# Raw halves in front of the root: leading units of three normed products in a two-block transformer kernel

## What is computed

```python
def rms_norm_2(x, g):
    xf = x.astype(jnp.float32)
    y = xf * lax.rsqrt(jnp.mean(xf * xf, axis=-1, keepdims=True) + EPS)
    return (y * g.astype(jnp.float32)).astype(x.dtype)

def modulate(h, shift, scale):
    return h * (1.0 + scale[:, None, :]) + shift[:, None, :]

def swiglu(h, w_gate, w_up, w_down):
    return (jax.nn.silu(h @ w_gate) * (h @ w_up)) @ w_down

# per layer i:
    h = modulate(rms_norm_2(x, ffn_norm[i, 0]), mod[:, 0, 0], mod[:, 0, 1])
    x = x + 0.5 * mod[:, 0, 2][:, None, :] * swiglu(h, ...)
    h = modulate(rms_norm_2(x, mix_norm[i]), mod[:, 1, 0], mod[:, 1, 1])
    y = conv_mixers(h, ...)       # layer 0; pool_moba_mixers(h, ...) in layer 1: z = h @ w_in, then u, q, k, v
    x = x + mod[:, 1, 2][:, None, :] * y
```

## Time and profile before

| | us |
|---|---|
| median of 3 runs | 1812.28 |
| lowest and highest | 1807.25, 1812.35 |
| the profiled execution | 1812.7 |
| its span | 1810.9 |

### The profile page before, as it was taken

The page is one execution under the profiler, slowest core; times in us unless marked ns, Lnnn a source line. Parts: engine busy times, 40 slices in busy tenths (PEclk is TensorE's granted clock), DMA queues, the critical chain, the costliest instruction groups (busy, mean ns, idle before and its releaser), DMA issues.

```text
span 1810.9 us, 34579 instructions
## 1 busy us (share of the span) xinstructions
PE 1766.4 (98%) x14098; PEld 1570.8 (87%) x14098; DVE 1380.5 (76%) x2297; ACT 1032.2 (57%) x1747; POOL 85.3 (5%) x163
## 2 busy tenths in 40 slices
PE   7999999989999999999999999999999999999998
PEld 6888889888888888888888888888888888988887
DVE  4758888767766478888888967688979887767664
ACT  3557764667766577654655412655555555466553
POOL 0000001100000000001001100010100010000000
PEclk9999999999999999999999999999999999999999
DMA  5356558443332356568788933788968887536552
GB/s 193 94 186 205 190 200 325 128 141 118 119 96 95 116 183 204 187 221 316 266 282 286 348 117 116 257 295 285 332 239 309 277 318 243 171 118 210 190 192 94
DMA packets 102827, 374.04 MB, mean 207 GB/s; under 512 B 11440, under 2 KB 11600, under 8 KB 102544
## 3 DMA queue, kind: packets, MB, share of 16 engines
q1 hardware_dynamic: 80352, 289.77, 46.8%
q0 software_dynamic: 22320, 82.09, 13.5%
HBM read 370.74 MB, written 1.08 MB: 205 GB/s over the span
## 4 chain that ended last, share of the span: by engine, by line
PE 92%; ACT 3%; DVE 3%; issue 1%; DMA 0%; SPq 0%; DVEq 0%; ACTq 0%
PE ps L520 40%; PE ps L523 22%; PE ps L2169 4%; PE ps L527 3%; PE ps L528 3%; PE ps L529 3%; PE ps L611 2%; PE ps L898 2%; PE ps L1083 1%; PE ps L2195 1%; PE ps L1264 1%; PE ps L1265 1%; PE ps L1266 1%; PE ps L317 1%; PE ps L1384 1%
## 5 line engine op out<-in xcount | busy, mean ns | idle before, releaser
L491 DVE TENSOR_TENSOR weights_lo<-weight_ring,weights_hi 128x1024 fp32r<-128x1024 f32 x493 | 602.3, 1223 | 158.3 <-ACT weights_hi L484 157.3
L484 ACT ACTIVATE weights_hi<-weight_ring 128x1024 fp32r<-128x1024 f32 x493 | 517.4, 1054 | 196.8 <-PE ps L520 120.2
L520 PE MATMUL ps<-u_halves,weights_hi 128*128 128x512 f32 x2176 | 536.7, 391 | 2.3 <-DVE u_halves L379 1.8
L520 PEld LDWEIGHTS ps<-u_halves,weights_hi 128*128 128x128 f32 x2176 | 400.3, 188 | 83.5 <-DVE u_halves L379 3.4
L523 PE MATMUL ps<-u_halves,weights_lo 128*128 128x256 f32 x2176 | 304.5, 283 | 0.0
L523 PEld LDWEIGHTS ps<-u_halves,weights_lo 128*128 128x128 f32 x2176 | 288.1, 191 | 10.1
L520 PE MATMUL ps<-act_halves,weights_hi 128*128 128x512 f32 x952 | 231.3, 391 | 0.0
L520 PEld LDWEIGHTS ps<-act_halves,weights_hi 128*128 128x128 f32 x952 | 173.5, 188 | 32.4
L721 DVE SCALAR_TENSOR_TENSOR ffn_tiles<-ffn_tiles,cond 128x1024 f32<-128x1024 f32 x144 | 175.4, 1220 | 3.0 <-DMA ffn_tiles<-in_ada 2.8
L633 ACT ACTIVATE ffn_tiles<-ps 128x512 f32<-128x512 f32 x136 | 80.8, 594 | 157.6 <-PE ps L523 157.4
L527 PE MATMUL ps<-u_halves,weights_hi 128*128 128x256 f32 x488 | 147.3, 302 | 4.9 <-DVE u L1887 2.9
(11 more groups left out here) (312 smaller groups left out, 2148.2 us busy)
## 6 DMA issues: line engine op xcount, KB each, us to landing
weight_ring<-in_w SPq DMA_DIRECT2D x545, 512.0 KB, 4.1
ffn_tiles<-in_ada POOLq DMA_DIRECT2D x144, 512.0 KB, 5.4
scaled<-gates_scratch POOLq DMA_DIRECT2D x8, 512.0 KB, 5.5
arena<-in_alibi POOLq DMA_DIRECT2D x1, 1536.0 KB, 6.9
h<-in_x SPq DMA_DIRECT2D x4, 256.0 KB, 3.9
out<-u SPq DMA_DIRECT2D x4, 256.0 KB, 2.4
consts<-in_consts SPq DMA_DIRECT2D x1, 592.0 KB, 10.2
cond<-in_cond SPq DMA_DIRECT2D x1, 512.0 KB, 11.2
```

Of the source, the lines that this page charges most:

```text
L484: nc.scalar.activation(w_slot(s)[0], ring[:, n % RING], ACT.Copy).then_inc(hi_ready, 1)
L491: nc.vector.tensor_tensor(lo, ring[:, n % RING], hi.bitcast(F32), ALU.subtract).then_inc(lo_ready, 1)
L520: return nc.tensor.matmul(ps[:, bank], hi, halves, start=start, stop=stop, skip_group_check=True)
```

## The change

At norms 4, 7 and 8 (`RAW`) the first four units (SPLIT) are multiplied with halves of h times norm weight, without the root. `lead_hi_act` makes the high half in the place of `scaled`, `lead_lo_dve` the low half right behind the sum of squares of the same chunk. The halves of the shift stand as columns 256 and 257 of the same tiles (`PITCH` = 258), so the products (`lead_pe`) have 258 columns, three for each chunk of a unit, and one unit follows another. Behind the fifth chunk of the first unit stands `norm_pe`, now with all eight squares summed on DVE and one ones-matmul, without warming matmuls. The results are multiplied by `rstd` on DVE (`lead_scale_dve`; in `moba_dve` in place in PSUM) and the shift's product is added as a bias (in the Silu, in `mul_dve`, in the pool copy). `norm_dve` and `norm_halves_act` still make the normed halves, which units 4 and on use. The fourth unit's weights are split before the root; the fifth's high half stands between chunks 3 and 4 of `norm_halves_act`. `ADA_DOWN` moves modulation sums away from the last chunk.

The diff, cut to its core:

```diff
+        RAW = (4, 7, 8)
+        GAIN_WITH_ROOT = (0, 1, 9) + RAW
+        AFTER = {3: 1, 4: 2, 6: 3, 7: 4, 8: "pm_in"}
...
+        def lead_hi_act(act, k, c):
+            if c == 0 and k in MODS:
...
+                nc.scalar.activation(lead_halves(k)[:, :, 0, T:PITCH], shift, ACT.Copy).then_inc(shift_hi_ready, 1)
+            nc.scalar.activation(lead_halves(k)[:, c, 0, 0:T], h[:, c], ACT.Copy, scale=norm_gain(k, c)).then_inc(lead_hi_ready, 1)
...
+            dve.wait_ge(lead_hi_ready, leads_until(k, c))
+            nc.vector.scalar_tensor_tensor(lead[:, c, 1, 0:T], h[:, c], norm_gain(k, c), lead[:, c, 0, 0:T].bitcast(F32),
+                                           ALU.mult, ALU.subtract).then_inc(lead_lo_ready, 1)
...
+        def lead_pe(pe, k):
...
+            for j in range(SPLIT):
+                s = split_wait(pe, AFTER[k], j)
+                pe.wait_ge(h_ready, C * (k - 1) + lead_bank_read(k, j))
+                for c in range(C):
+                    if j == 0:
+                        pe.wait_ge(lead_lo_ready, leads_until(k, c))
+                    nc.tensor.matmul(ps[:, j, 0:n], w_hi[:, s, c], lead[:, c, 0, 0:n], start=c == 0, stop=False, skip_group_check=True)
+                    nc.tensor.matmul(ps[:, j, 0:n], w_hi[:, s, c], lead[:, c, 1, 0:n], start=False, stop=False, skip_group_check=True)
+                    last = nc.tensor.matmul(ps[:, j, 0:n], w_lo[:, s, c], lead[:, c, 0, 0:n], start=False, stop=c == C - 1, skip_group_check=True)
+                    if j == 0 and c == SUM_BEHIND:
+                        norm_pe(pe, k)
+                last.then_inc(unit_done, 1)
+
+        SUM_BEHIND = 4
...
         def norm_halves_act(act, k):
             for c in range(C):
+                if k in RAW and c == C // 2:
+                    split_hi(act, AFTER[k], SPLIT)
...
+        ADDED.update((k, C) for k in RAW)
...
-            if k in WARM:
+            if k in WARM and k not in RAW:
                 warm_pe(6, WARM[k])
...
-        ADA_DOWN = [[3] + [2] * 6 + [1]] * 2 + [[3] * 3 + [2] * 4 + [1], [3] + [2] * 6 + [1], [2] * 4 + [1] * 4, [0] * C]
+        ADA_DOWN = [[3] + [2] * 6 + [1], [3] * 2 + [2] * 5 + [0], [3] * 3 + [2] * 4 + [1], [3] + [2] * 6 + [0], [2] * 6 + [1] + [0], [0] * C]
...
         def corr_act(act, q, f):
+            if f < 2 and k_raw(q):
+                return
...
+            if k + 1 in RAW:
+                split_hi(act, AFTER[k + 1], SPLIT - 1)
             norm_root_act(act, k + 1)
...
+        def lead_scale_dve(dve, q, f):
+
+            unit_products(dve, FIRST_UNIT[f"ffn{q}"], 2 * f + 1)
+            if FFN[q][0] in MODS:
+                nc.vector.tensor_copy(lead_bias[:, 2 * f:2 * f + 2], ps[:, 2 * f:2 * f + 2, T])
+            root2 = rstd[:].unsqueeze(1).to_broadcast([P, 2, T])
+            nc.vector.tensor_tensor(gu[:, f % 3], ps[:, 2 * f:2 * f + 2, 0:T], root2, ALU.mult).then_inc(gu_ready, 1)
...
                 add_squares_dve(dve, k + 1, c - 1)
+                if c and k + 1 in RAW:
+                    lead_lo_dve(dve, k + 1, c - 1)
                 ffn_residual_dve(dve, steps, q, c)
...
+            if k + 1 in RAW:
+                add_squares_dve(dve, k + 1, C - 1)
+                lead_lo_dve(dve, k + 1, C - 1)
             if piece > bias_from:
                 mods_bias_dve(dve, bias_from, piece)
+            if k + 1 in RAW:
+                split_lo(dve, AFTER[k + 1], SPLIT - 1)
...
         def moba_pe(pe):
...
+            lead_pe(pe, 8)
+            for n in range(SPLIT, 12):
...
                 if n == 8:
+                    pe.wait_ge(p_copied, 4)
                     scores_pe(pe, 1, 0)
...
                 if n < 4:
+                    if n:
+                        split_hi(act, "pm_in", n + 4)
+                    act.wait_ge(p_scaled, n + 1)
+                    nc.scalar.activation(px[:, n, PADP:PADP + T], ps[:, n, 0:T], ACT.Identity, bias=lead_bias[:, n:n + 1]).then_inc(p_copied, 1)
+                    continue
...
+            split_lo(dve, "pm_in", 4)
+            for n in range(SPLIT):
+                unit_products(dve, FIRST_UNIT["pm_in"], n)
+                nc.vector.tensor_copy(lead_bias[:, n:n + 1], ps[:, n, T:T + 1])
+                nc.vector.tensor_tensor(ps[:, n, 0:T], ps[:, n, 0:T], rstd[:], ALU.mult).then_inc(p_scaled, 1)
+                if n == 1:
+                    split_lo(dve, "pm_in", 5)
+            split_lo(dve, "pm_in", 6)
+            split_lo(dve, "pm_in", 7)
```

More of the change, by code:

```diff
@@ L130, in build @@
         u = sb("u", [P, C, T])
+        PITCH = T + 2
+        with nc.sbuf_tensor("lead_in_mix", [P, C, 2, PITCH], FR) as lead_in_mix:
+            pass
         with nc.sbuf_tensor("mix_halves", [P, 2 * C, T], FR) as mix_halves:
@@ new lines, in lead_bank_read @@
+        def lead_bank_read(k, j):
+            if k == 3:
+                return 2 * j + 2
+            if k == 6:
+                return (7, 8, 2, 4)[j]
+            return 5 + j
+        def lead_pe(pe, k):
+            lead, n = lead_halves(k), PITCH if k in MODS else T
+            if k in MODS:
+                pe.wait_ge(shift_lo_ready, shifts_until(k))
+            for j in range(SPLIT):
[10 more added lines that the diff above has]
+                last.then_inc(unit_done, 1)
@@ L394, in residual_dve @@
                 split_lo(dve, next_ffn, 0)
+            raw = k + 1 in RAW
             for c in range(C):
-                if banks != "lin":
+                if banks != "lin" and not raw:
                     add_squares_dve(dve, k + 1, c - 1)
@@ L559, in ffn_up_pe @@
                         begin, end = first and c == 0, not first and c == C - 1
+                        if j == SPLIT and first and k in RAW:
+                            pe.wait_ge(u_hi_ready if part == "low" else u_lo_ready, 8 * HALVES_OF[k] + c + 1)
+                        elif j == SPLIT and k in RAW:
+                            pe.wait_ge(u_lo_ready, 8 * HALVES_OF[k] + c + 1)
                         if part == "high":
@@ L621, in ffn_pe, with k_raw, corrs_until @@
             ffn_down_pe(pe, q)
-            norm_pe(pe, FFN[q][0] + 1)
+            if FFN[q][0] + 1 not in RAW:
+                norm_pe(pe, FFN[q][0] + 1)
         def has_split(q, j):
             return j < 3 * FFN[q][1] + {0: GDN_SPLIT, 1: SPLIT - 1, 3: SPLIT - 1, 4: SPLIT - 1}.get(q, 0)
+        def k_raw(q):
+            return FFN[q][0] in RAW
+        def corrs_until(q, f):
+            return F_BASE[q] + f + 1 - 2 * sum(k_raw(i) for i in range(q + 1))
         def corr_act(act, q, f):
+            if f < 2 and k_raw(q):
+                return
             unit_products(act, FIRST_UNIT[f"ffn{q}"], 2 * f + 1)
@@ L644, in silu_act @@
                 act.wait_ge(act_ready, n - 2)
-            nc.scalar.activation(sgb[:, f % 2], src, ACT.Silu).then_inc(sg_ready, 1)
+            bias = lead_bias[:, 2 * f:2 * f + 1] if f < 2 and k_raw(q) and FFN[q][0] in MODS else 0.0
+            nc.scalar.activation(sgb[:, f % 2], src, ACT.Silu, bias=bias).then_inc(sg_ready, 1)
         def act_hi_act(act, q, f):
@@ L2490, in moba_dve @@
                 m(nc.vector.memset(b[:, :, 0:PADP], 0.0))
-            for n in range(4, 8):
-                split_lo(dve, "pm_in", n)
+            split_lo(dve, "pm_in", 4)
[7 more added lines that the diff above has]
+            split_lo(dve, "pm_in", 7)
             w()
```

105 lines of the change are left out of this document (71 added, 34 removed).

## The result

| | before | changed |
|---|---|---|
| median, us | 1812.28 | 1802.15 |
| lowest and highest of 7 runs, us | 1807.25, 1813.72 | 1798.79, 1803.63 |
| ratio, with its 95% interval | | 0.9945 [0.9935, 0.9956] |
| span of the profiled execution, us | 1810.9 | 1800.4 |
| mean granted clock | 0.995 | 0.996 |

What follows compares the result with a forecast made beforehand. PE's stream of products and its stops were taken as the bound. Savings of 3.35, 3.4 and 3.1 us at norms 4, 7 and 8, taken as 9.8, gave 1802.9 from 1812.7, then 1802.5 us for the runs; range 1797.5 to 1809.5.

Steps and rivals of the forecast that it cites:

- What bounds the kernel: PE's stream of products plus its stops; at norms 4, 7 and 8 together 12.83 us pass without a product.
- The products: Four lead units at each norm: 96 products of 258 columns at 0.121 us, 11.6 us against 11.14 at norms 4 and 7.
- Rival B: The 288 lead products of 258 columns are slower than rows of 256, up to +29 us, 1831 us; chance 0.07.
- Unit 0: First lead unit: PE does not stop, with 0.2 us to spare at the sum and 1 us at step 7.
- PE is free at 1337.84: At norm 7, after the last down product: the time from which the lead was taken to start.
- Rival C: The sum of squares inside unit 0 stops PE; 1 us per norm returns, 1805.5 us; chance 0.08.
- Unit 4: First unit on normed halves, the tightest place: PE waits about 0.15 us; 3.35, 3.4 and 3.1 us saved at norms 4, 7, 8.
- The root: On ACT, unit 3's split put before the root costs nothing, since the ones-matmul releases the root at the same time, 1340.4.
- Unit 5 at norm 8: ACT waits for the scaled pool input before it splits unit 5: another 0.1 us.
- Moved load: Extra DVE work in the down stages, 3.2 us each, and moved modulation sums: costed at nothing; without cover up to 3.2 us per norm.
- rival A: DVE takes the chain's place, in down stages or at unit 4's weights: 1.5 to 3.2 us per norm; chance 0.13.
- The total: Whole kernel: 9.8 us off the profiled 1812.7 gives 1802.9, with the runs' median 0.4 lower, 1802.5 us.

Runs made afterwards that it cites:

- experiments 1 to 3: Kernel before with only the change's SBUF addresses, 1811.82 us, ratio 1.0004; then the changed kernel with the lead at fewer norms, raw78 and raw8.
- Experiment 7: Changed kernel with tiles of pitch 256 and the lead as products of 512 and 256 columns, without the shift: 1803.75 us, ratio 0.996 to the kernel before.
- experiment 8: Changed kernel with each low half of the lead made twice on DVE, once into an unread tile: 1803.96 us, ratio 0.9954 to the kernel before.
- experiment 4: Changed kernel with the ones-matmul behind the eighth chunk of unit 0 in place of the fifth: 1804.53 us, ratio 0.9962 to the kernel before.
- Experiment 6: Changed kernel with unit 4's low half made before DVE's eighth norm chunk and, at norm 8, unit 5 split before the first pool copy: 1801.47 us.
- after_again: The changed kernel measured once more, nothing altered: 1803.63 us against 1810.88 for the kernel before, ratio 0.9956.
- raw78: Changed kernel with the lead at norms 7 and 8 only, norm 4 put back: 1804.6 us against 1811.3 for the kernel before, ratio 0.9971.
- raw8: Changed kernel with the lead at norm 8 only, norms 4 and 7 put back: 1808.04 us against 1811.3 for the kernel before, ratio 0.9978.

## Why the prediction was right, and where it was not

**What bounds the kernel**: right. PE's stream was stopped in the three stretches, and the gain is found at the norms that have the lead and nowhere else (experiments 1 to 3). One loss elsewhere, between norms 5 and 6, comes below.

**The products**: 288 products of 258 columns at 0.121 us were predicted; the lead takes 12.09 us with its ones-matmul (1333.48 to 1345.45 and one product more), against 12.1. Rival B, slower products, is excluded. Experiment 7 adds what the prediction didn't see: their price was not on the path at all, for unit 4 starts at the same time with the cheaper form. The price was also too high. In experiment 7 it is 0.17 us a lead in place of 0.46, since products of 512 and 256 columns that alternate take 0.354 us a step (21 steps from 1342.46 to 1349.89, before) and 0.357 in experiment 7, and not the 0.348 of the groups in rows 8. The sum didn't suffer, for it compares with the measured 11.37 us.

**Unit 0**: predicted 0.2 us of margin for the sum of squares and no stop. The profile names no stop, but the margin is gone: the ones-matmul is released by the sum, 0.08 us late at norm 7 (experiment 8). The step at fault is "PE is free at 1337.84". PE was free 0.18 us earlier, and the lead reaches the sum that much sooner. Rival C did not happen, but its place is real and close.

**Unit 4** was named the tightest place, and it is. The prediction has unit 4 start at 1350.1, 13.40 us behind the start of the last down products; measured are 13.43, 13.48 and 13.65. That fits at norms 4 and 7, where 3.35 and 3.4 us were predicted and 3.32 came, but with luck, for terms are off and nearly cancel. The lead starts 0.18 us earlier than was taken. PE stops for 0.43 us and not 0.15. And DVE's norm is longer: 6.6 us from the trace of before plus 0.6 for the inserted split, 7.2, and measured are 7.38 (1337.28 to `half_gate`'s start at 1344.66). The 6.6 were of `norm_dve` on `scaled`, a TENSOR_TENSOR of 0.42 us. With the lead there is no `scaled` made on ACT, and the diff shows it: `GAIN_WITH_ROOT` takes in `RAW`, so the operation becomes a SCALAR_TENSOR_TENSOR with the gain, 0.48 us (L435), 0.40 from start to start (1338.80 to 1339.20) in place of 0.34 (0.42 less the overlap of 0.08). Eight times 0.06 is 0.5 us, and it was in the diff to be read. The inserted split, on the other hand, delayed DVE by 0.34 us (before 1342.00) and not by 0.6. The two misses, +0.5 and -0.26, are about the 0.2 us by which the norm is longer; it starts 4.76 us behind the last down products where 4.85 was predicted.

At norm 8, where 13.78 was predicted (1539.2 - 1525.42), unit 4 starts after 13.65, and the start before was taken 0.16 us too early (1542.38 for 1542.54): 3.47 us in place of the 3.2 that the prediction has before it takes off 0.1 for unit 5.

**The root**: "that insertion costs nothing: the two end together" was right. In experiment 4, where nothing else holds it, the root starts 0.63 us after the ones-matmul (1333.26 to 1333.89), here 0.71, so the split holds it by at most 0.1; and rstd is ready 0.25 us before DVE can use it.

**Unit 5 at norm 8**: predicted 0.1 us late. The stretch from norm 8 to the end gained 3.10 us where unit 4's start has 3.47, so 0.4 was given back behind it. The profile names no wait there, but the starts show it: unit 5's first product is 0.15 us late, where 0.1 was predicted, and the second product behind each stop costs 0.10 more. Experiment 6 gets all of it back, 0.9 us with the 0.60 before unit 4.

**Moved load**, costed at nothing in the down stages: right, with a cover that is used up at twice the load (rival A's price shows at norm 7 only, in experiment 8). Not right on one point that the sum didn't have: in the stage between norms 5 and 6 the changed kernel loses 0.4 to 0.5 us. It is 105.4 and 105.3 us (after_again) against 104.9, and 104.6 in raw78 and raw8, whose sums for the modulation are placed as in the changed kernel. There PE has one new wait, in the mixer between these norms:

```profile
1089.25 1.12 PE L2318 MATMUL ps<-arena,consts 128*128 128x512 f32 x2 [0.41 <-DVE arena L2409]
```

It appears with 0.3 to 0.4 us in all six profiles of kernels with a lead at norm 4, and neither before nor in raw78 or raw8. In five of the six the wait before the mixer's first product (for ACT) is also 0.7 us in place of 0.4; in the sixth, two_products, it isn't, and there the stage takes 105.0. What makes DVE and ACT late there was not tried, and stays open.

**The total**: 1802.5 predicted, 1802.15 measured, and this agreement is better than the working behind it. By the stages the norms gave 9.6 us in place of 9.85, the mixer took 0.4 to 0.5 back, and the stretch before norm 4 gave 1.45 us that the change has no part in. Without that the gain is 9.05 us, and the profiled execution would have taken 1803.65 us, against 1802.9 that the sum gave: an error of some 0.75 us. The second measurement of the same kernel, 1803.63 us, lies there, 7.25 us below its own runs of before (1810.88), where the first lies 10.13 below.

## What to carry to other kernels

Where an engine shows 98% busy, look at what the busy time is made of: three stretches of 4.3 us were filled with matmuls that nobody read, and products that don't need the result being waited for took their place. Once such a gap is closed, the end is set by what was hidden behind it, here DVE's norm and one weight half: count it with the operations of the changed code, not with those of the trace before, and look there first for the next gain (some 0.5 us at norms 4 and 7 by moving one instruction). Judge steps of this size by stages between fixed points, since the totals of this kernel scatter by more than a step brings.
